# Encoder step on one core: attention scores on 64 partitions in place of a zero-padded query, and layers written out

## The reference

```python
qa, ka, va, qb, kb, vb = jnp.split(u @ w_in[l], 6, axis=-1)
qa = qa.reshape(B, T, HA, DHA)           # group A: 8 heads of 64
qb = qb.reshape(B, T, HB, 2, DHB)        # group B: 4 heads, two maps of 64 each
...
s = jnp.einsum('bcqhd,bckhd->bchqk', qc, kb) * DHA ** -0.5 + bias          # A, band
...
s = jnp.einsum('bqhid,bkhid->bihqk', qblk, k) * DHB ** -0.5                # B
s = s - slopes[:, None, None] * dist
p = jax.nn.softmax(s, axis=-1)
a = p[:, 0] - lam * p[:, 1]
```

## Time and profile before

| | |
|---|---|
| median of three runs | 2848.67 us (2848.31 to 2850.84) |
| span of the profiled execution | 2849.9 us |
| share of the span: PE, PEld, DVE, ACT, POOL | 91%, 86%, 47%, 31%, 5% |
| chain that ended last: PE, DVE, issue, ACT | 80%, 10%, 4%, 3% |
| mean granted clock of PE | 0.966 of 2.4 GHz |
| own attention, both layers | about 637 to 800 and 2024 to 2187 us |

### The profile page before, as it was taken

The page is one execution under the profiler, slowest core; times in us unless marked ns, Lnnn a source line. Parts: engine busy times, 40 slices in busy tenths (PEclk is TensorE's granted clock), DMA queues, the critical chain, the costliest instruction groups (busy, mean ns, idle before and its releaser), DMA issues.

```text
span 2849.9 us, 50460 instructions
## 1 busy us (share of the span) xinstructions
PE 2590.2 (91%) x19353; PEld 2444.8 (86%) x19353; DVE 1325.4 (47%) x2185; ACT 896.4 (31%) x1493; POOL 153.1 (5%) x262
## 2 busy tenths in 40 slices
PE   5999997999887879999989999989988887999995
PEld 4999997986587679999989999989756866999995
DVE  4444325345846564442264442353466655444325
ACT  3222223224533432222232232232343434222222
POOL 2000001001101010000010000010110001000001
PEclk8999999999989999999999999999998998999997
DMA  5323332331023123233222233323311311322321
GB/s 151 89 88 88 94 91 80 113 109 45 23 82 102 33 60 88 88 90 89 80 60 85 85 96 92 101 62 116 98 33 41 93 60 32 94 84 86 101 82 56
DMA packets 386066, 230.94 MB, mean 81 GB/s; under 512 B 6668, under 2 KB 373278, under 8 KB 385920
## 3 DMA queue, kind: packets, MB, share of 16 engines
q1 hardware_dynamic: 380352, 207.64, 24.7%
q0 software_dynamic: 4368, 16.92, 1.7%
q10 hardware_dynamic: 1200, 4.46, 0.4%
HBM read 215.44 MB, written 18.79 MB: 82 GB/s over the span
## 4 chain that ended last, share of the span: by engine, by line
PE 80%; DVE 10%; issue 4%; ACT 3%; DMA 2%; POOL 0%; DVEq 0%; ACTq 0%; SPq 0%; POOLq 0%
PE psum L588 70%; PE psum L741 3%; DVE x L1111 3%; PE psum L564 3%; PE psum L760 2%; ACT u_hi L942 1%; DVE w_lo L1116 1%; PE psum L762 1%; DVE y_mix L1149 1%; DMA bias_tab_dram<-bias_rev_dram 1%; DVE r_pre L1122 1%; PE psum L754 1%; ACT w_hi L901 1%; DVE u_lo L1111 1%; DMA w_raw<-in_w_ffn_gu 0%
## 5 line engine op out<-in xcount | busy, mean ns | idle before, releaser
L588 PE MATMUL psum<-u_hi,w_hi 128*128 128x272 f32 x4096 | 867.4, 293 | 106.6 <-DVE u_lo L1111 82.9
L588 PE MATMUL psum<-u_hi,w_lo 128*128 128x272 f32 x4096 | 857.3, 291 | 0.0
L588 PE MATMUL psum<-u_lo,w_hi 128*128 128x272 f32 x4096 | 854.9, 291 | 0.0
L588 PEld LDWEIGHTS psum<-u_hi,w_hi 128*128 128x128 f32 x4096 | 654.1, 192 | 121.0 <-DVE u_lo L1111 93.8
L901 ACT ACTIVATE w_hi<-w_raw 128x1024 fp32r<-128x1024 f32 (+1 forms) x338 | 378.7, 1120 | 1129.9 <-PE psum L588 1118.4
L588 PEld LDWEIGHTS psum<-u_lo,w_hi 128*128 128x128 f32 x4096 | 654.5, 192 | 0.0
L588 PEld LDWEIGHTS psum<-u_hi,w_lo 128*128 128x128 f32 x4096 | 650.0, 192 | 0.0
L1116 DVE TENSOR_TENSOR w_lo<-w_raw,w_hi 128x1024 fp32r<-128x1024 f32 (+1 forms) x338 | 439.0, 1299 | 366.9 <-ACT w_hi L901 362.0
L588 PE MATMUL psum<-h_hi,w_lo 128*128 128x272 f32 x1408 | 291.5, 288 | 0.0
L588 PE MATMUL psum<-h_hi,w_hi 128*128 128x272 f32 x1408 | 291.1, 288 | 0.0
L588 PE MATMUL psum<-h_lo,w_hi 128*128 128x272 f32 x1408 | 290.3, 288 | 0.0
(11 more groups left out here) (176 smaller groups left out, 2261.0 us busy)
## 6 DMA issues: line engine op xcount, KB each, us to landing
w_raw<-in_w_ffn_gu SPq DMA_DIRECT2D x178, 512.0 KB, 3.8
w_raw<-in_w_ffn_dn SPq DMA_DIRECT2D x64, 704.0 KB, 4.5
w_raw<-in_w_in SPq DMA_DIRECT2D x48, 512.0 KB, 3.8
w_raw<-in_w_out SPq DMA_DIRECT2D x16, 512.0 KB, 3.7
w_raw<-in_w_ckv SPq DMA_DIRECT2D x16, 512.0 KB, 3.7
bias_tab_dram<-bias_rev_dram POOLq DMA_DIRECT2D x1, 5120.0 KB, 22.1
table<-bias_tab_dram SPq DMA_DIRECT2D x16, 320.0 KB, 3.0
out<-k_nat POOLq DMA_DIRECT2D x4, 1024.0 KB, 5.0
```

The lines of the kernel that those rows point to most:

```text
L588: pe_last[0] = pe.matmul(psum[:, bank + half, 0:c1 - c0], w, xx[:, c0:c1], start=s0, stop=s1)
```

## The change

Scores of own attention read the 64 partitions that belong to the head, of query, key and cached key alike. `q_pad`, its memset, its semaphore and POOL's copies are gone, and with them the waits of PE. POOL's second value store now follows straight on the second key store. The layer loop is written out on all five engines, so the layer number is a constant. Loops inside the feed-forward stages stay.

```diff
@@ schedule()
-                        s["pad"] = (side, len(padded[side]) % 2)
-                        s["pad_free"] = padded[side][-2] if len(padded[side]) >= 2 else None
-                        padded[side].append(s["slot"])
+                        s["side"] = side
@@ the same on sync, tensor, scalar, vector and gpsimd
-        with sp.Fori(0, DEPTH) as l:
+        for l in range(DEPTH):
@@ gpsimd, in a layer
             store_keys(l, 1, *k_outs[1])
-            pool.wait_ge(qk_kept, l * 16 + 16)
-            settled(pool)
-            for it in SLOT_USERS:
-                if "pad" in it:
-                    pad_query(l, it)
-                    if it["biased"] == 5:
-                        store_values(l, 1, *v_outs[1])
+            store_values(l, 1, *v_outs[1])
@@ tensor, score()
-            pe.wait_ge(q_padded, l * TOTAL["biased"] + it["biased"] + 1)
-            q = q_pad[:, it["pad"][0], it["pad"][1], 0:rows]
-            k = qk[:, base + 4 + tile, :]
+            part = slice(64 * it["side"], 64 * it["side"] + 64)
+            q = qk[part, base + tile, frames]
+            k = qk[part, base + 4 + tile, :]
             if i < NT:
                 return pe.matmul(slot_ap(slot, rows, keys_of(u)), q, k[:, 0:keys_of(u)], start=True, stop=True)
             pe.wait_ge(cache_kept, l * TOTAL["cache"] + cached)
-            pe.matmul(slot_ap(slot, rows, PAST), q, kc_t[:, tile, :], start=True, stop=True)
+            pe.matmul(slot_ap(slot, rows, PAST), q, kc_t[part, tile, :], start=True, stop=True)
             return pe.matmul(slot_ap(slot, rows, SAMPLE, PAST), q, k[:, SEQ:T], start=True, stop=True)
```

More of the change, by code:

```diff
@@ L68, in schedule @@
     slot_users = []
-    padded = ([], [])
     probs_owner = {}
@@ L195, in build @@
     headinv = place("headinv", [128, 4 * (NT + 1)])
-    q_pad = place("q_pad", [128, 2, 2, 128])
     dist = place("dist", [128, TABW])
@@ L296, in build @@
     cross_tile, setup_vals, gains_now, rowinverted = sem("cross_tile"), sem("setup_vals"), sem("gains_now"), sem("rowinverted")
-    q_padded = sem("q_padded")
     passed, warm_done = sem("passed"), sem("warm_done")
@@ L472, in _ @@
                   allow_small_or_imprecise_dtypes=True).then_inc(dist_ready, 1)
-        pool.memset(q_pad[:, :, :, :], 0.0).then_inc(consts, 1)
         pool.memset(masktile[:, :], MASKED).then_inc(consts, 1)
@@ L481, in _ @@
         pool.wait_ge(tab_made, 16)
-        pool.wait_ge(consts, 4)
+        pool.wait_ge(consts, 3)
         pool.dma_start(tab_dram[:, 0:64, 576:640].rearrange("t p w -> p t w"),
@@ L516, in store_values @@
             pool.dma_start(sample[l], v_nat[0:SAMPLE, NT, g * 512:(g + 1) * 512]).then_inc(v_stored, 16)
[L518 to L524, removed]
-                settled(pool)
-            pool.tensor_copy(q_pad[part, side, place_, 0:rows], qk[part, tile, u["i"] * 128:u["i"] * 128 + rows]
-                             ).then_inc(q_padded, 1)
         k_outs = [(fl(p_a_k), fl(s_a_k)), (fl2(p_b_k), fl2(s_b_k))]
@@ L531, in _ @@
         sum_x_squares(0)
-        with pool.Fori(0, DEPTH) as l:
+        for l in range(DEPTH):
             sum_x_squares(4 * l + 1)
@@ L761, in score @@
             pe.wait_ge(cache_kept, l * TOTAL["cache"] + cached)
-            pe.matmul(slot_ap(slot, rows, PAST), q, kc_t[:, tile, :], start=True, stop=True)
+            pe.matmul(slot_ap(slot, rows, PAST), q, kc_t[part, tile, :], start=True, stop=True)
             return pe.matmul(slot_ap(slot, rows, SAMPLE, PAST), q, k[:, SEQ:T], start=True, stop=True)
         pe.wait_ge(iden, 2)
-        pe.wait_ge(consts, 4)
+        pe.wait_ge(consts, 3)
         pe.wait_ge(setup_loaded, 80)
@@ L781, in _ @@
         pe.wait_ge(setup_vals, 5)
-        with pe.Fori(0, DEPTH) as l:
+        for l in range(DEPTH):
             base = l * PAIRS
@@ L1035, in _ @@
         next_input(0, 8)
-        with act.Fori(0, DEPTH) as l:
+        for l in range(DEPTH):
             base = l * PAIRS
@@ L1342, in _ @@
             low_input(0, k, 8)
-        with dve.Fori(0, DEPTH) as l:
+        for l in range(DEPTH):
             base = l * PAIRS
```

## The result

The changed kernel takes 2877.41 us, the median of four runs (2864.61 to 2887.56), against 2849.76 us for the kernel before on the same chip: a ratio of 1.0086, with a 95% interval of 1.0054 to 1.0118. The forecast was 2857.3, with a range to 2866. Its sign came true, the size did not. A ratio leaves out the runs that are more than 1.5% above the fastest of their kernel, a median does not.

What follows compares the result with a forecast made beforehand. PE was taken to bound group A, DVE group B. From span 2849.9: +11.9 (A forms) -1.4 (A constants) +0 (B) -3.9 (loop) +2.0 (store) = +8.6, 2858.5; carried to the median, 2857.3 us; range 2843 to 2866, its own 2852 to 2862.

Steps and rivals of the forecast that it cites:

- The product itself takes as long: its time goes by columns: Group A scores: a 64-row product costs the same time as before, 0.108 us for 128 columns.
- forms in A: Group A scores on 64 rows: added changes of PE form cost 1.49 us per two heads, +11.9 us in both layers.
- constants in A: Group A, sample score's bias: constants instead of registers save 0.7 us a layer, -1.4 us in both.
- group B: Own attention bound by DVE: form changes +1.8 and constants -1.8 us a layer, so it comes out even.
- loop written out: Layer boundary and first layer's entry: the jump and ACT table loads go, -3.9 us together, bounds -2.0 and -4.5.
- store moved: POOL's value store overlaps the wait for cached keys: 1.0 us a layer, +2.0 us, bounds 0 and 3.2.
- The rival by which the 64-row form is free: Scores of A and B: the 64-row form costs nothing, -6.9 us, 2841.8 us; chance 17%.
- the second rival: Group B: form changes cost, but its two maps run side by side, +5.0 us, 2853.7 us; chance 14%.
- The boundary: From last residual tile to layer 1's steady products: 14.31 us without a loop closing against 16.62, 2.3 us saved.
- The first layer's entry: First layer, first to steady products: 12.39 us against 10.75, 1.6 us saved, one table load behind `norm_sum`.
- Register instructions in the feed-forward stages: Feed-forward stages: PE follows on itself there, so register instructions cost nothing.
- The lower bound, 0: Moved value store at the wait for cached keys: lowest cost 0, against 1.0 us a layer taken.

Runs made afterwards that it cites:

- nine later ones: The changed kernel itself measured again in nine runs, nothing altered: 2854.05 to 2903.66 us, median 2893.27, 1.0154 over the median of the kernel before.
- the kernel with three padded heads: Changed kernel with value store at its old place and heads 0, 1 of A and 0 of B padded to 128 rows: 2840.07 us, 0.9970.
- unrolled padded kernel: Kernel before with only the layer loop written out, scores still over 128 partitions with the padded query: 2837.30 us, 0.9946.
- the fill over 128 rows: Changed kernel plus dummy products over 128 rows ahead of the third cached-key tile, five in A, three in B: 2846.04 us, 0.9978.
- that over 64 rows: Changed kernel plus dummy products over 64 rows ahead of the third cached-key tile, five in A, three in B: 2877.90 us, 1.0085.

## Why the prediction was wrong, point by point

The step that failed is the sentence "The product itself takes as long: its time goes by columns". At 2.4 GHz that is so. But the sum was made for the clock of the kernel before, and no term and no rival asked what 64 rows do to the clock, though the earlier trace rows shows it at 0.50 in the very wait ahead of the first scores. That term is 33 us by the ratios of the first four runs, and more by the nine later ones. Without it the kernel would have been *faster*, as the kernel with three padded heads is (0.9970 [0.9960, 0.9980]): that the direction came true is luck. The other terms, by ratios and by the chain at full clock:

| term | forecast | measured |
|---|---|---|
| forms in A | +11.9 | 8 pairs of heads x (21.60 - 20.38) = +9.8 |
| constants in A | -1.4 | 8 x (20.38 - 20.46) = -0.6, stands in the line of the loop |
| group B | +3.6 forms, -3.6 constants | 8 x -0.27 = -2.2 with 64 rows; the constants, 8 x -0.76 = -6.1, stand in the next line |
| loop written out | -3.9 | with all that constants for registers give: -15.4 |
| store moved | +2.0 | 0 |
| clock | none | +33 |

The lines add up to 25 us, the ratio gives 24.5.

*Changes of form in A: right.* The timeline of PE after the change, to set beside the earlier trace rows:

```profile
687.53 0.91 PE L737 MATMUL psum<-qk 64*128 64x384 f32 x2
688.37 0.33 PE L541 MATMUL psum<-ident,probs 128*128 128x128 f32 x1
688.63 1.06 PE L718 MATMUL psum<-vc,probs_t 128*32 128x128 f32 x8
689.62 0.40 PE L718 MATMUL psum<-v_nat,probs_t 32*32 32x128 f32 x2
689.95 1.12 PE L737 MATMUL psum<-qk 64*128 64x512 f32 x2
691.01 0.83 PE L541 MATMUL psum<-ident,o_nat 128*128 128x128 f32 x5
```

The score of 384 columns now lasts 0.84 us from start to start instead of 0.65, 0.19 more for its two borders at this place; the one of 512 lasts 1.06 instead of 0.96, one border more. Two heads take 21.60 us against 20.46, where 22.0 less 0.2 was forecast; against the 20.38 of the unrolled padded kernel, whose constants are the same, it is 1.22 for the 1.49 forecast. The rival by which the 64-row form is free falls here.

*Group B: wrong by 8 us.* Its terms were to cancel. The gap ahead of a bias is gone (0.12 us in the earlier trace rows); on DVE after the change:

```profile
772.68 0.08 DVE L1282 DVE_READ_ACCUMULATOR2_ANT headsq<- 128x1 f32 x1
772.72 0.56 DVE L1229 CUSTOM_DVE_ANT_0 probs<-psum,table 128x384 f32<-128x384 f32 x1
```

0.04 us lie between the starts, where the earlier trace rows have 0.20 (756.11 to 756.31): 0.16 less, not 0.09. The forecast counted from the end of the short read, but the bias now starts before that end. Two heads of B before the change, by the chain:

```profile
743.85 1.32 PE psum L741 x10
...
773.31 1.32 PE psum L741 x10
```

29.46 us, 14.73 a head. In the unrolled padded kernel a head:

```profile
753.86 1.32 PE psum L741 x10
...
767.83 1.32 PE psum L741 x10
```

13.97, 0.76 less, where 0.45 was forecast. The distance from that read to the bias accounts for it: over the five units of a head it adds up to 1.00 us before (756.11 to 768.35) and to 0.27 in the unrolled padded kernel. With 64 rows it falls once more, to 13.7 (771.44 to 785.14), since there the second rival happened too. From the timeline of PE after the change:

```profile
773.87 1.13 PE L737 MATMUL psum<-qk 64*128 64x512 f32 x4
774.93 0.44 PE L541 MATMUL psum<-ident,square 128*128 128x128 f32 x2
```

Four passes of 512 columns, two on each half of the array, take 1.06 us from start to start. The same four before the change:

```profile
745.10 1.99 PE L760 MATMUL psum<-qk,q_pad 128*128 128x512 f32 x4
746.92 0.38 PE L564 MATMUL psum<-ident,probs 128*128 128x128 f32 x2
```

They took 1.82. That is the rule of the Trainium skill on side by side row groups (TensorE: Matmul & The Clock Gate, Packing small matmuls), and the rows now confirm it. It is worth 0.27 us a head only, since DVE sets the pace in B, as forecast.

*The loop.* The boundary came out to 0.1 us: 14.3 forecast, and in the chain after the change, from the last residual tile to the steady products:

```profile
1454.73 1.80 DVE x L1088
...
1469.01 379.08 PE psum L565 x3024
```

14.28 us against 16.62. The first layer's entry fell short: from the products that start at 57.81 in the earlier trace rows to the steady ones it is 11.60 us (55.89 to 67.49) instead of 12.39, 0.8 less where 1.6 was forecast, since a table load of 1.28 us still stands in the chain there (58.09). The 2.7 us of the table of stages have 1.9 from ahead of these products. Register instructions in the feed-forward stages were set at nothing, and the other stages are together 8.0 us shorter; but 4.3 of these are clock. The kernel before has a dip late in layer 1 (192 products of the chain in 27.06 us, here 24.33) and one at the first steady products (380.65 us in the earlier trace rows, here 379.09), and the latter comes and goes between kernels: with the fill over 128 rows it is 380.63, with that over 64 rows 379.10. Where the other 3.7 us lie, and so how much of the 15.4 is register instructions and how much chance of the clock, isn't shown.

*The store.* The wait for cached keys was to grow from 4.8 to 5.8 us. It is 4.48:

```profile
630.92 1.94 PE L541 MATMUL psum<-ident,kc_nat 128*128 128x128 f32 x8 [4.48 <-DMA kc_nat<-in_cache_a_k]
```

POOL issued the store at 628.58, and the keys came no later. The lower bound, 0, was the right value.

*What stays open.* By what rule the clock comes back, and why the same kernel is down for 14 us behind one wait (layer 1 of the first profiled run) and for 90 behind another (layer 0 of the second): no experiment controlled that. The looped kernel with 64-row scores wasn't run, nor the moved store alone; the share of the 64 rows alone is read from the changed against the unrolled padded kernel.

## What to carry to other kernels

Before replacing a zero-padded product by one over fewer rows, look at the granted clock around it: if PE comes out of a wait there at 1.2 GHz, the padding may be what brings the clock back, and it is cheap. Price a change of form at some 0.1 us out and 0.1 in, and put the products that need 128 rows first after a wait, or fill the wait with dummies over 128 rows, which helps less surely (two of ten runs of the changed kernel stayed long). And when the runs of a kernel scatter and the longer have the lower mean clock, list the clock by windows before reading waits: at half speed PE showed no idle time (80.00 of 80 us busy).

## What the runs showed of the hardware

- At 1.2 GHz with PE busy 80.00 of 80 us: the clock stays down under unbroken work with scores over 64 rows among it. With dummies over 64 rows after 2.19 us of idle time it fell from 1.00 to 0.50 while they ran, in both layers; over 128 rows it stayed at 1.00. Straight behind dense work, or after 0.35 us, it stayed at 1.00 over 64 rows too.
- Full products over 64 rows on different halves of the array run side by side in fp32: 1.06 us for 4 x 512 columns against 1.82.
- Dummy products in the two waits for cached keys made own attention of the padded kernel 4.8 and 1.2 us shorter in the profiled runs, which the ratios don't resolve (0.9946 and 0.9941). Three more a layer in another wait brought 3.6 us on one chip (2831.74 to 2828.16 us).
- Writing a loop of two passes out brought 0.54%, more than its jump: 2.3 us at the boundary, 0.16 us ahead of each unit's first bias where DVE is the bound, and a part that is not assigned.
